# A ring of three weight slots in place of four, outside the experts of a two-model, four-layer step

## The reference, cut to what matters

```python
x = x + g1 * token_mixer(h, ...)        # h @ w_in, o @ w_branch, y @ w_out
f = (silu(h @ w1) * (h @ w3)) @ w2      # layer 0: D_FF = 2816
f = sum_e comb[:, e] * swiglu(t, w1[e], w3[e], w2[e])   # layer 1: 8 experts
# second model, both layers
u = causal_depthwise_conv(h @ w_up); a, b = split(u); y = (silu(a) * b) @ w_down
```

## Time and profile before

| | us |
|---|---|
| runs | 2756.14, 2754.90, 2752.39 |
| median | 2754.9 |
| span of the profiled execution | 2752.1 |
| TensorE busy | 2702.7 (98%) |
| VectorE busy | 968.5 (35%) |
| ScalarE busy | 528.4 (19%) |
| moved by DMA | 706.6 MB, mean 257 GB/s |

### The profile page before, as it was taken

The page is one execution under the profiler, slowest core; times in us unless marked ns, Lnnn a source line. Parts: engine busy times, 40 slices in busy tenths (PEclk is TensorE's granted clock), DMA queues, the critical chain, the costliest instruction groups (busy, mean ns, idle before and its releaser), DMA issues. The chain is left out here.

```text
span 2752.1 us, 45257 instructions
## 1 busy us (share of the span) xinstructions
PE 2702.7 (98%) x19261; PEld 2104.4 (76%) x19261; DVE 968.5 (35%) x2203; ACT 528.4 (19%) x1128; POOL 93.7 (3%) x181
## 2 busy tenths in 40 slices
PE   7999999999989999999999999999999999999999
PEld 6788988978878645555555548787988997879888
DVE  2655432376620000000000105575565245644330
ACT  3322100233210001101101103423112024231110
POOL 0000110000100000000000000000011000000000
PEclk9999999999989999999999999999999999999999
DMA  9536675555479989999999985335576543324432
GB/s 377 198 126 245 247 265 217 227 193 182 160 308 426 398 334 395 426 426 408 426 426 408 425 357 223 138 123 187 210 279 237 203 171 138 114 101 161 168 115 100
DMA packets 70327, 706.62 MB, mean 257 GB/s; under 512 B 7792, under 2 KB 8048, under 8 KB 31600
## 3 DMA queue, kind: packets, MB, share of 16 engines
q1 hardware_dynamic: 44640, 610.92, 55.4%
q0 software_dynamic: 25488, 92.81, 9.6%
HBM read 702.65 MB, written 1.05 MB: 256 GB/s over the span
## 5 line engine op out<-in xcount | busy, mean ns | idle before, releaser
L989 PE MATMUL psum<-hT,ring 128*128 128x256 f32 x4544 | 994.4, 380 | 0.0
L989 PEld LDWEIGHTS psum<-hT,ring 128*128 128x128 f32 x4544 | 860.1, 190 | 121.3 <-ACT work L1595 2.0
L989 PE MATMUL psum<-work,ring 128*128 128x256 f32 x1624 | 357.5, 382 | 11.0 <-DVE hT L1854 11.0
L989 PEld LDWEIGHTS psum<-work,ring 128*128 128x128 f32 x1624 | 311.0, 192 | 55.4 <-DVE hT L1854 11.8
L2294 DVE CUSTOM_DVE_ANT_0 mod_in<-mod_in,c_rows,cols 128x1024 f32<-128x1024 f32 x152 | 190.8, 1279 | 38.2 <-DMA mod_in<-in_mods 34.7
L1250 PE MATMUL psum<-ring,work 128*32 128x256 f32 x2880 | 186.5, 381 | 0.0
L2255 DVE TENSOR_TENSOR work<-work,psum 128x128 f32<-128x128 f32 x119 | 34.3, 288 | 413.9 <-ACT work L1636 413.9
L2421 POOL DMA_DIRECT2D mod_in<-in_mods x176 | 93.0, 529 | 2478.9 <-DVE ada L2294 2433.2
L1004 PE MATMUL psum<-hT,ring 128*128 128x128 f32 x1408 | 162.7, 277 | 3.0 <-DVE hT L1907 1.9
L1004 PEld LDWEIGHTS psum<-hT,ring 128*128 128x128 f32 x1408 | 161.0, 193 | 3.7 <-DVE hT L1907 2.0
L1260 PE MATMUL psum<-ring,work 128*64 128x256 f32 x1280 | 147.0, 382 | 0.0
(11 more groups left out here) (262 smaller groups left out, 2474.5 us busy)
## 6 DMA issues: line engine op xcount, KB each, us to landing
ring<-in_m SPq DMA_DIRECT2D x112, 2048.0 KB, 16.3
work<-in_m SPq DMA_DIRECT2D x56, 2048.0 KB, 17.4
ring<-in_w_in SPq DMA_DIRECT2D x46, 2048.0 KB, 8.4
mod_in<-in_mods POOLq DMA_DIRECT2D x176, 512.0 KB, 5.4
ring<-in_up SPq DMA_DIRECT2D x22, 2048.0 KB, 8.2
ring<-in_f SPq DMA_DIRECT2D x11, 2048.0 KB, 8.8
ring<-in_down SPq DMA_DIRECT2D x16, 1408.0 KB, 6.5
ring<-in_w_o SPq DMA_DIRECT2D x8, 2048.0 KB, 8.6
```

Source lines behind the costliest of these rows:

```text
L989: last = mm(gbank(it["bank"])[:, j, :], wt[:, k, col0 + j * P:col0 + (j + 1) * P], rhs[:, k0 + k, :], start=(n == 0), stop=(n == total - 1))
```

## The change

Outside the experts chunk n goes into slot n % 3 in place of n % 4, with three semaphores slot_loaded in place of four. The tile keeps its four slots of room, and the experts' ring its six blocks at the same addresses. The units, their order and SP's order of loads stay.

```diff
-RING = 4
+RING = 3
+RING_ROOM = 4
...
-        ring = sb("ring", [P, RING, SLOT])
+        ring = sb("ring", [P, RING_ROOM, SLOT])
...
-        blocks = [ring[:, i, :] for i in range(RING)] + [work[:, off + i * SLOT:off + (i + 1) * SLOT]
-                                                         for i in range(ROUND_RING - RING)]
-        assert off + (ROUND_RING - RING) * SLOT <= WN
+        blocks = [ring[:, i, :] for i in range(RING_ROOM)] + [work[:, off + i * SLOT:off + (i + 1) * SLOT]
+                                                              for i in range(ROUND_RING - RING_ROOM)]
+        assert off + (ROUND_RING - RING_ROOM) * SLOT <= WN
```

## The result

The changed kernel takes 2783.88 us (median of four runs, 2781.94 to 2784.98) against 2755.52 us; the ratio is 1.0106, 95% interval 1.0094 to 1.0118. That is 28.4 us more where I had forecast 21. The profiled execution took 2784.98 us, with a span of 2782.8 us, 30.7 us more than the span of before.

The account below looks back on a forecast made before the run. TensorE, busy for 98% of the span, was taken as the bound; 10.9 us full-unit waits, 7.7 split-unit waits and 2.4 clock loss make 21.0, so 2754.9 goes to 2776 us; spread 2769 to 2781, wider range 2769 to 2785.

Parts of the forecast that it names:

- The experts, and the chunks used one at a time: Experts' ring and dense weights with one chunk in use: three slots still hide the loads, 0 us.
- The nine waits: Units 1 to 3 of three down projections wait for their second chunk: seven of 1.55 us, two split of 3.85.
- SP's order of issue stays: In SP's queue: loads are only issued one chunk later, and nothing else moves; no cost was given.
- The Trainium skill's fit: Landing of a down chunk: 2.0 us plus bytes over 436 GB/s, 5.3 us; set aside for the rows' 5.9 to 6.0.
- The clock behind the waits: TensorE's lower clock after the two split units' waits: 1.2 us each, 2.4 in all; 0 after the short waits.
- rival (a): Down projections: TensorE's clock falls in all nine waits, giving 2791 us; chance 0.09.
- Rival (b): Down projections: two transfers issued at a unit's end share the engines, landing about 8.0 us, giving 2792 us; chance 0.06.
- (c): Down projections: the second chunk comes in time for full units, so not slower, 2759 us; chance 0.05.
- (d): Whole kernel: the change does nothing, as the ring isn't where its depth bites, 2755 us; chance 0.02.
- The POOL queue's loads of mods feed VectorE, not TensorE, and keep their issue times relative to the units: 0.: Mods loads beside the dense weights: three slots cost TensorE nothing through them, 0 us.
- the rest of the span keeps its length within 2 us: Sign to look for: start, experts and projections outside the down stretches change by no more than 2 us.
- The start: First loads: the fourth first_mods chunk, issued later, still lands at 27.0 us; between -1 and +1 us, taken as 0.

Follow-up runs that it names:

- both4: Changed kernel, but f2, down and the first model's layer 1 w_pa, w_pb and w_o go round four slots; 2754.76 us, ratio 0.9999.
- ring2: Changed kernel with two ring slots in place of three; 2871.71 us, ratio 1.0421.
- shift: Changed kernel with mods pieces in the first model's layer 1 mixer spread over units 2 to 25, not 2 to 29; 2779.23 us, ratio 1.009.
- mix4: Changed kernel, but w_pa, w_pb and w_o of the first model's layer 1 go round four slots; 2778.4 us, ratio 1.0081.
- fill_again: Second series of the changed kernel with eight idle matmuls ahead of the wait in each of the two split down-projection units; 2784.48 us.
- again: The changed kernel run once more, without any further change; 2783.67 us.
- down3: Kernel before, with four slots, but the chunks of f2 and down go round three; 2781.44 us, ratio 1.0097.

## Why the prediction held, and where it didn't

**The experts, and the chunks used one at a time: right.** both4 and ring2 show both: no loss outside the two places, and hardly one with one slot less still.

**The nine waits: right in place and number, and nearly in size.** Forecast 10.9 us for the seven full units and 7.7 for the split ones. The list puts each wait some 0.3 us shorter than what its unit grew by (1.00 against 1.27 us at f2's second unit); counted in full the split ones waited 3.9 us each, 7.8. By SP's issue times the full units grew by 1.3 and 1.6 in f2, 1.6 and 1.5 in down of layer 0, 1.6, 1.4 and 2.5 us in the last down: 11.5 us. The last is the one that stands out, and its cause is a thing that I had said couldn't happen: "SP's order of issue stays" is true, yet what lies behind the load moved. SP's timeline at that unit's start:
```profile
2757.68 0.33 SPq L900 DMA_DIRECT2D ring<-in_down  x1
2758.05 1.58 SPq L939 DMA_DIRECT2D xT_out<-xT  x3
```
and the landing of that load:
```profile
DMA to landing us min/median/max: 6.9/6.9/6.9
```
In the kernel before, the last load left at 2710.88 and the stores of the result went out one by one as units ended. Now the last load waits until unit 2 has ended, three of the four stores queue up behind it and go out together 0.4 us after it, and it lands at 6.9 us and not at 5.8 to 6.0. That the stores are what slows it fits the rows and wasn't tried.

**The Trainium skill's fit** ("DMA: Bandwidth & Descriptors", the anatomy of one DMA) gave an estimate of 5.3 us per chunk; measured 5.7 to 6.0 again. The section gives the fit for transfers issued from GpSimd, and SP issues these, which the prediction didn't say. The row of before was the better price.

**The clock behind the waits: right in kind, short in size.** For the split units I took 1.2 us each. The rows at 0.50 behind the waits of 3.6 us in the changed kernel (us, TensorE's busy time and records, clock, DMA):
```profile
500.60:504.10 3.50, 3.50 (x17) 0.51 1.00 426
2208.70:2214.10 5.40, 5.35 (x25) 0.50 0.71 303
```
At full clock these records take 17 x 0.11 and 25 x 0.11: 1.6 and 2.6 us lost, 4.2 in place of 2.4. The bounds I gave were 0 to 2.4 each; the larger one passes them. The first half of the split unit grew to 15.8 and 16.7 us, where I had written 14 to 15. Behind the seven waits of 1.0 to 2.3 us no row is at 0.50 in either trace of the changed kernel, so rival (a) fell as a case of all nine. The border isn't sharp, though, on either side: in shift the wait of 3.7 us in down of layer 0 had no spell of low clock behind it, and in mix4 the longest of the seven, 2.3 us in the last unit, did have a spell of 3.4 us behind it, as had the one of 2.5 us in fill_again. The two windows of mix4, the records after the wait and the spell:
```profile
2758.15 5.19 PE L996 MATMUL psum<-work,ring 128*128 128x256 f32 x15 [2.30 <-DMA ring<-in_down]
...
2758.80:2762.20 3.40, 3.40 (x10) 0.50 0.14 54
```

**Rival (b), the pair sharing the engines, fell:** 5.7 and 9.8 us are one behind the other. (c) and (d) fell with the nine waits.

**The step that failed: "The POOL queue's loads of mods feed VectorE, not TensorE, and keep their issue times relative to the units: 0."** Both halves are true up to the collision, and the conclusion is wrong. Mods keep their times, but the weights' transfers move by a chunk relative to them, and VectorE in its order carries a late piece over to the evacuation of a PSUM bank that TensorE needs. Measured: 3.2 us of wait, some 1.8 us lost in the spell of low clock that starts at 736.2 behind it (the 16 records from 735.39 to 740.63 take 5.2 us where 16 x 0.216 is 3.5), and a few small ones, 5.4 us in the profiled run; 5.5 us between the medians of the changed kernel and mix4, 4.7 against shift (4.4 with again, which ran beside shift, in its place). I had asked what SP's loads are moved past in SP's own queue, and not on the DMA engines that both queues share. With this the sign "the rest of the span keeps its length within 2 us" failed as well: outside the down projections 7.4 us were added. The forecast's 21.0, 5.4 here, 1.8 more of clock and 0.6 more of waits make 28.8, against 28.4 between the medians.

**What was luck.** The wider range reached to 2785 us for a part of rival (a), low clock behind the short waits. That isn't what happened. The 5.4 us of the mods and the clock behind the split waits filled the same room, so that the median fell into the range says less for the prediction than the nine waits do.

**The start** ended 1.2 us later in this trace. down3, which has four slots at the start as the kernel before has, shows such a delay too (its matmuls on the fourth first_mods chunk are 1.3 us later, TensorE's "issue" wait there 2.9 us). And with three slots at the start the first matmuls on w_in begin at 33.4 to 36.8 us in the eleven traces that have them, five of them before the 34.8 us of the kernel before. So this is the spread of executions and not the change.

## What to carry to other kernels

Count a ring's depth by the greediest user, not by the typical one: a unit that holds m chunks at once needs 2m slots to be fetched one unit ahead, and with one slot less it waits for landing minus the work it can do without the missing chunk. That subtraction, done with a landing that the trace before already holds, came within 1 us of what the nine waits cost together and gave 6.3 us for waits of 6.0 to 6.6 with two slots. Working off the first chunk completely before touching the second, and freeing it at once, buys the slot back for a second PSUM bank and no time that could be measured. And when loads are moved in time, list every transfer of the other queues in the new stretch, and what stands behind its consumer on that engine: here it was the evacuation that frees a PSUM bank.

## What the runs showed that I hadn't expected

- A 512 KB piece that lands in 4.4 to 5.1 us by itself took 9.8 to 10.9 us beside a 2048 KB chunk from the other queue, and the chunk took 10.9 us. The trace of before has the same at another place, 9.4 and 9.8 us.
- Waits of 3.4 to 3.6 us were followed by 3.4 to 6.8 us of clock 0.50 in both traces of the changed kernel; the waits for c1 up to 1.6 us never were, and those of 2.2 to 2.5 us sometimes; one of 3.7 us, in shift, wasn't either. Idle matmuls in the wait kept the clock up in both traces that had them, and the launch's time didn't show it clearly.
- With two slots in place of four the dense weights used one at a time still hide: the loss of 116 us lies nearly whole in and just behind 12 units of the down projections.
